# Gated delta-net: q and k normalised while v is projected, first decays early, TensorE past a barrier

## The reference

```
proj = h @ w_in                                  # h is rms-normed, 1024 wide
qkv = silu(causal_conv(proj[:, :4096], 4 taps))  # q 8 heads, k 8 heads, v 16 heads of 128
q = l2_norm(q) * 128 ** -0.5; k = l2_norm(k)     # x * rsqrt(sum(x * x) + 1e-6) over a head
beta = sigmoid(b); g = -exp(a_log) * softplus(a + dt_bias)
o = chunk_gated_delta_rule(q, k, v, g, beta)     # chunks; decay = exp(cum_i - cum_j), i >= j
out = (rms_norm(o) * silu(z)) @ w_out            # z is a further 2048 columns of proj
```

## Time and profile before

| what | value |
|---|---|
| median of three runs | 2754.71 us (2752.78 to 2757.27) |
| the profiled execution | 2757.49 us |
| its span in the profile | 2755.6 us |
| mean granted clock of TensorE | 0.931 |
| TensorE busy | 2570.0 us |
| VectorE busy | 1409.2 us |
| ScalarE busy | 849.9 us |

### The profile page before, as it was taken

How to read it: one execution, slowest core, us unless ns; L and a number is a source line. 1 busy time by engine, 2 the same in 40 slices (tenths; PEclk the granted TensorE clock), 3 DMA queues, 4 the chain that set the end, 5 groups by cost and what they waited for, 6 DMA issues and landing times.

```text
span 2755.6 us, 40042 instructions
## 1 busy us (share of the span) xinstructions
PE 2570.0 (93%) x16152; PEld 2254.5 (82%) x16152; DVE 1409.2 (51%) x1925; ACT 849.9 (31%) x1251; POOL 237.1 (9%) x186
## 2 busy tenths in 40 slices
PE   6998999888999999989997999998997788899998
PEld 6997999888999999989886888886884445688886
DVE  6676655552554443542464666766216364534433
ACT  5322443434332222322222322223223354322322
POOL 1000222220010000100100100002003100100001
PEclk9997999896999999999886999998997899899999
DMA  3222433332122222222101344543220000122221
GB/s 127 82 86 66 104 87 81 85 68 79 62 91 93 84 85 91 92 93 77 46 0 46 128 162 168 185 152 105 100 92 16 0 0 15 61 100 98 91 92 62
DMA packets 91971, 230.92 MB, mean 84 GB/s; under 512 B 59994, under 2 KB 61612, under 8 KB 67668
## 3 DMA queue, kind: packets, MB, share of 16 engines
q1 hardware_dynamic: 86320, 197.04, 22.3%
q10 hardware_dynamic: 5540, 32.30, 3.4%
HBM read 217.67 MB, written 11.64 MB: 83 GB/s over the span
## 4 chain that ended last, share of the span: by engine, by line
PE 84%; DVE 9%; ACT 3%; issue 2%; DMA 1%; DVEq 0%; ACTq 0%; POOL 0%; POOLq 0%; SPq 0%
PE ps L289 64%; PE ps L453 2%; PE ps L479 1%; PE ps L967 1%; PE ps L293 1%; PE ps L2173 1%; PE ps L950 1%; PE ps L960 1%; PE ps L2155 1%; DMA g_EC<-scr_g 1%; PE ps L1622 1%; PE ps L1623 1%; DVE a_mx L2239 1%; DVE g_tmp L1114 1%; PE ps L979 1%
## 5 line engine op out<-in xcount | busy, mean ns | idle before, releaser
L289 PE MATMUL ps<-xa_hi,whi 128*128 128x264 f32 (+1 forms) x2512 | 654.5, 320 | 44.0 <-DVE wlo L312 19.9
L289 PE MATMUL ps<-xa_lo,whi 128*128 128x264 f32 (+1 forms) x2512 | 650.3, 318 | 0.0
L289 PE MATMUL ps<-xa_hi,wlo 128*128 128x264 f32 (+1 forms) x2512 | 648.9, 318 | 0.0
L312 DVE TENSOR_TENSOR wlo<-raw,whi 128x2048 fp32r<-128x2048 f32 x161 | 370.6, 2302 | 257.7 <-ACT whi L305 257.7
L289 PEld LDWEIGHTS ps<-xa_hi,whi 128*128 128x128 f32 x2512 | 418.6, 191 | 86.1 <-issue 32.5
L305 ACT ACTIVATE whi<-raw 128x2048 fp32r<-128x2048 f32 x161 | 307.5, 1910 | 581.4 <-PE ps L289 577.0
L289 PEld LDWEIGHTS ps<-xa_hi,wlo 128*128 128x128 f32 x2512 | 417.7, 191 | 29.8
L289 PEld LDWEIGHTS ps<-xa_lo,whi 128*128 128x128 f32 x2512 | 417.7, 191 | 29.3
L289 PE MATMUL ps<-xb_hi,whi 128*128 128x264 f32 (+1 forms) x1280 | 385.3, 342 | 7.4 <-DVE xb_lo L1739 5.6
L289 PE MATMUL ps<-xb_lo,whi 128*128 128x264 f32 (+1 forms) x1280 | 386.1, 342 | 0.0
L289 PE MATMUL ps<-xb_hi,wlo 128*128 128x264 f32 (+1 forms) x1280 | 384.3, 341 | 0.0
(11 more groups left out here) (387 smaller groups left out, 2954.1 us busy)
## 6 DMA issues: line engine op xcount, KB each, us to landing
raw<-weights SPq DMA_DIRECT2D x161, 1024.0 KB, 4.9
mod_w<-weights_mod ACTq DMA_DIRECT2D x24, 1024.0 KB, 4.9
g_EC<-scr_g SPq DMA_DIRECT2D x10, 424.0 KB, 5.1
scr_z<-z_st SPq DMA_DIRECT2D x16, 264.0 KB, 4.6
g_D<-scr_g SPq DMA_DIRECT2D x10, 371.0 KB, 5.1
scr_a<-g_AT SPq DMA_DIRECT2D x10, 318.0 KB
h<-x_in ACTq DMA_DIRECT2D x4, 528.0 KB, 8.1
z_a<-scr_z SPq DMA_DIRECT2D x4, 528.0 KB, 4.9
```

The source lines that it names most:

```text
L289: mm = pe.matmul(ps[:, at_ + step * c + bank, 0:tn], w[:, hb.slot, k, c * P:(c + 1) * P], x[:, k, t0:t0 + tn], start=(k == 0 and n == 0), ...
L312: dve.tensor_tensor(wlo[:, hb.slot], raw[:, hb.raw_slot], whi[:, hb.slot].bitcast(F32), ALU.subtract).then_inc(S("w_lo"), 1)
```

## The change

The l2 norm is no step of its own any more. Its statistics (`dve_l2_stats`) stand behind the first half block of v, (4,0); its transposes (`pe_l2_rows`) in the middle of the second tile of (4,1); its roots (`act_l2_roots`) behind (4,1), and the low part (`dve_l2_low`) ahead of (5,0). The 16 columns of the identity are copied at once into `head_one`. From the tile (5,0,1) to (7,0,0) each projection tile has a slot of two heads behind it on TensorE (`pe_l2_tiles`); VectorE multiplies the two heads (`dve_l2_tiles`) right behind the evacuation of the next projection tile. The loops over v's half blocks are written out. ScalarE issues the masks' DMAs behind the roots, and ends the first step with the decays of half 0 and the split of half block 18, whose VectorE part moves behind `matrices(0)`. GpSimd clears its tiles early and ends the first step with the differences of half 0. TensorE doesn't wait at the first barrier (`join=st.n > 0`): it goes on with kk(0) and two z half blocks and waits behind them. SyncE's first transfers for the delta rule stand ahead of the load of half block 18, and the load of 19 behind `blocks_in(0)`.

Left out below are the removal of the turn-0 cases in `pe_headnorm` and `dve_headnorm` (`head_all` and `head_out` raised by two), a wait for the norm ahead of the masks' DMAs, and `decays` and `differences` under their new names `act_row_decays` and `pool_differences`, otherwise the same.

```diff
--- before.py
+++ after.py
@@ -152,7 +152,8 @@
         misc = con.take("misc", [P, 8])
         stat = con.take("stat", [P, 8])
         head_stat = con.take("head_stat", [P, 96])
-        head_st = [con.take(f"head_st{c}", [P, 8], F32R) for c in range(2)]
+        head_one = con.take("head_one", [P, 16], F32R)
+        head_st = [head_one[:, 8 * c:8 * c + 8] for c in range(2)]
         xa_hi = at("xa_hi", [P, KT, T], SB_XA, F32R)
         xa_lo = at("xa_lo", [P, KT, T], SB_XA + X_BYTES, F32R)
         xb_hi = at("xb_hi", [P, KT, T], SB_XB, F32R)
@@ -234,10 +235,15 @@
...
-            def end(self):
+            def end(self, join=True):
 
                 self.eng.drain().then_inc(S("stage_" + self.name), 1)
                 self.n += 1
+                if join:
+                    self.join()
+
+            def join(self):
+
                 for other in ENGINES:
                     if other != self.name:
                         self.eng.wait_ge(S("stage_" + other), self.n)
@@ -666,8 +668,10 @@
             return HalfBlock(HB_GDN_IN, i, 2).after(s) if not isinstance(i, int) else HalfBlock(HB_GDN_IN + 2 * i + s)
 
         def pe_gdn_in(pe):
-            def project(i, s):
-                pe_hb(pe, gdn_hb(i, s), xa_hi, xa_lo, FULL, "conv_x", i * 4 + 2 * s)
+            pe.sem_inc(S("head_all"), 2)
+
+            def project(i, s, during=None, between=None):
+                pe_hb(pe, gdn_hb(i, s), xa_hi, xa_lo, FULL, "conv_x", i * 4 + 2 * s, during=during, between=between)
 
             def sums(i, s, ahead=0):
 
@@ -689,10 +693,63 @@
             pe_gdn_gates(pe)
             project(HALF_IN, 0)
             sums(HALF_IN, 1, ahead=4)
-            project(HALF_IN, 1)
-            with pe.Fori(HALF_IN + 1, 2 * HALF_IN) as i:
-                project(i, 0)
-                project(i, 1)
+            project(HALF_IN, 1, during=((1, KT // 2), lambda: pe_l2_rows(pe)))
+            for i in range(HALF_IN + 1, 2 * HALF_IN):
+                for s in range(2):
+                    project(i, s, between=lambda: pe_l2_tiles(pe, i, s, 0))
+                    pe_l2_tiles(pe, i, s, 1)
+
+        L2_FIRST = 4 * HALF_IN + 5
+
+        def l2_tiles(i, s, c):
+
+            slot = 4 * i + 2 * s + c - L2_FIRST
+            return range(2 * slot, 2 * slot + 2) if 0 <= slot < 8 else ()
+
+        def pe_l2_rows(pe):
+            chunks, size = token_chunks(FULL)
+            pe.wait_ge(S("head_inv"), 2)
+            for j, (bank, a, _) in enumerate(chunks):
+                mm = pe.transpose(ps[0:16, 6 + bank, a:a + size], head_stat[0:size, 16 * j:16 * j + 16], ident[0:size, 0:size])
+            mm.then_inc(S("head_rows"), 1)
+
+        def pe_l2_tiles(pe, i, s, c):
+            pe.wait_ge(S("head_lo"), 1)
+            pe.wait_ge(S("head_st"), 16)
+            for n in l2_tiles(i, s, c):
+                pe.wait_ge(S("head_out"), n + 1)
+                for bank, t0, tn in FULL:
+                    for part in l2_roots[1:]:
+                        mm = pe.matmul(ps[:, 4 + 2 * (n % 2) + bank, 0:tn], head_one[0:16, n:n + 1].to_broadcast([16, P]), part[0:16, t0:t0 + tn],
+                                       start=part is l2_roots[1], stop=part is l2_roots[2])
+                mm.then_inc(S("head_all"), 1)
+
+        def act_l2_roots(act):
+            act.activation(head_one[0:16, :], ident[0:16, 0:16], ACT.Copy).then_inc(S("head_st"), 16)
+            act.wait_ge(S("head_rows"), 1)
+            for to in l2_roots[:2]:
+                act.activation(cols(to[0:16], FULL), ps[0:16, 6:8, 0:T // 2], ACT.Sqrt).then_inc(S("head_rstd"), 1)
+
+        def dve_l2_stats(dve):
+            chunks, size = token_chunks(FULL)
+            x = head_stat[0:size, 0:16 * len(chunks)]
+            dve.sem_inc(S("head_out"), 2)
+            dve.wait_ge(S("head_sums"), 16)
+            dve.tensor_scalar(x, ps[0:size, 4, 0:16 * len(chunks)], 1.0, EPS, ALU.mult, ALU.add).then_inc(S("head_inv"), 1)
+            dve.wait_ge(S("head_inv"), 1)
+            dve.reciprocal(x, x).then_inc(S("head_inv"), 1)
+
+        def dve_l2_low(dve):
+            root_, hi, lo = (x[0:16] for x in l2_roots)
+            dve.wait_ge(S("head_rstd"), 2)
+            dve.tensor_tensor(lo, root_, hi.bitcast(F32), ALU.subtract).then_inc(S("head_lo"), 1)
+
+        def dve_l2_tiles(dve, i, s, c):
+            for n in l2_tiles(i, s, c):
+                x = cols(qkv[:, n], FULL)
+                dve.wait_ge(S("head_all"), n + 3)
+                dve.scalar_tensor_tensor(x, x, prm("l2_gain", n), ps[:, 4 + 2 * (n % 2):6 + 2 * (n % 2), 0:T // 2], ALU.mult, ALU.mult)\
+                    .then_inc(S("head_out"), 1)
 
         def act_gdn_in(act):
             act.sem_inc(S("conv_silu"), 2)
@@ -724,11 +781,14 @@
...
-            with act.Fori(HALF_IN, 2 * HALF_IN - 1) as i:
+            for i in range(HALF_IN, 2 * HALF_IN):
                 for s in range(2):
-                    convolved(i, s, False)
-            for s in range(2):
-                convolved(2 * HALF_IN - 1, s, False, split=s == 0)
+                    convolved(i, s, False, split=(i, s) != (2 * HALF_IN - 1, 1))
+                    if (i, s) == (HALF_IN, 1):
+                        act_l2_roots(act)
+                        act_gdn_masks(act)
+            act_row_decays(act, 0)
+            act_split(act, HalfBlock(HB_GDN_OUT + 1))
 
         def dve_gdn_in(dve):
             dve.sem_inc(S("conv_out"), 2)
@@ -740,12 +800,14 @@
...
-            def convolved(i, s, split=True):
+            def convolved(i, s, split=True, also=None):
                 hb = gdn_hb(i, s)
                 for c in range(2):
                     dve.wait_ge(S("tiles_done"), hb.index * 2 + (c + 1))
                     dve.wait_ge(S("conv_out"), i * 4 + (2 * s + c + 1))
                     dve.tensor_tensor(cols(conv_in[:, c, 3:], FULL), pair(c, FULL), cols(rstd, FULL), ALU.mult).then_inc(S("conv_x"), 1)
+                    if also:
+                        also(c)
                     dve.wait_ge(S("conv_x"), i * 4 + (2 * s + c + 3))
                     dve.wait_ge(S("conv_silu"), i * 4 + (2 * s + c + 1))
                     for j in range(4):
@@ -768,11 +830,13 @@
...
-            with dve.Fori(HALF_IN, 2 * HALF_IN - 1) as i:
+            for i in range(HALF_IN, 2 * HALF_IN):
                 for s in range(2):
-                    convolved(i, s)
-            for s in range(2):
-                convolved(2 * HALF_IN - 1, s, split=s == 0)
+                    if (i, s) == (HALF_IN + 1, 0):
+                        dve_l2_low(dve)
+                    convolved(i, s, split=(i, s) != (2 * HALF_IN - 1, 1), also=(lambda c: dve_l2_tiles(dve, i, s - 1 + c, 1 - c)) if i > HALF_IN else None)
+                    if (i, s) == (HALF_IN, 0):
+                        dve_l2_stats(dve)
 
 
         def by_chunk(x):
@@ -984,27 +1049,30 @@
...
+            pe.wait_ge(S("head_out"), 16 + 2)
+            pe.wait_ge(S("conv_x"), 32 + 2)
             kk(0)
             for n in range(Z_EARLY):
                 z_block(n)
+            join()
...
@@ -1045,10 +1113,9 @@
...
-            decays(0)
             scaled(0)
             act_split(act, HalfBlock(HB_GDN_OUT + 2))
-            decays(1)
+            act_row_decays(act, 1)
             scaled(1)
@@ -1184,6 +1251,7 @@
             dve.sem_inc(S("z_ev"), 2)
             dve.wait_ge(S("in"), IN_FIRST + 32)
             matrices(0)
+            dve_split(dve, HalfBlock(HB_GDN_OUT + 1))
             z_out(0, 0)
@@ -1197,6 +1265,14 @@
...
+        def pool_differences(pool, t):
+            if t == 0:
+                pool.wait_ge(S("in"), IN_FIRST + 32)
+            pool.wait_ge(S("g_cum"), 16 * (t + 1))
+            for x in range(2):
+                d = heads4(g_D[t % 2], x)
+                pool.tensor_tensor(d, d, g_neg[0:CH, None, :].to_broadcast([CH, 4, CH]), ALU.add).then_inc(S("g_dif"), 1)
+
@@ -1278,7 +1346,6 @@
...
-            next_load(HB_GDN_OUT + 1)
             sp.wait_ge(S("gates_a"), 8)
@@ -1288,13 +1355,15 @@
...
             sp.wait_ge(S("g_set"), 16 * (N_BLK + 3))
+            sp.wait_ge(S("w_lo"), HB_GDN_OUT)
             cum_rows(0)
-            next_load(HB_GDN_OUT + 2)
+            next_load(HB_GDN_OUT + 1)
             for name in ENGINES:
-                sp.wait_ge(S("stage_" + name), 2)
+                sp.wait_ge(S("stage_" + name), 1)
             decay_rows(0)
             blocks_out(0)
             blocks_in(0)
+            next_load(HB_GDN_OUT + 2)
@@ -2318,9 +2387,9 @@
...
-                lambda: (pool_gdn_gates(pool), pool_norm(pool, 0, FULL)),
-                lambda: (pool.memset(g_diag[:, :, :], 0.0).then_inc(S("set"), 1), pool.memset(qkv[:, :, T:TP], 0.0).then_inc(S("set"), 1),
-                         pool.memset(g_S[:, :, :], 0.0).then_inc(S("set"), 1)),
+                lambda: (pool_gdn_gates(pool), pool_norm(pool, 0, FULL), pool.wait_ge(S("gates_z"), 2),
```

(14 more changed lines are left out.)

35 lines of the change are left out of this document (13 added, 22 removed).

## The result

| | before | after |
|---|---|---|
| median of the comparison (7 runs each), us | 2757.55 (2752.78 to 2763.97) | 2771.91 (2770.26 to 2779.36) |
| ratio | | 1.0055 (1.0041 to 1.0070) |
| profiled execution, us | 2757.49 | 2770.26 |
| its span, us | 2755.6 | 2768.5 |
| last projection tile of v ends, us | 241.09 | 279.07 |

The forecast was 2766.6 with a range of 2756 to 2774. The times shown ahead of it had a median of 2754.71; times the ratio that is 2769.9. The sign, the range and the place were right; the size was too small. The medians of the table differ by 14.4 us; the ratio makes it 15.2. At the place itself the change costs 318.38 - 301.46 = 16.9 us, where the forecast had 11.9.

The account below looks back on a forecast made before the run. TensorE, busy for 93% of the span, was taken as the bound. Slots and smaller terms less the hole gave +4.4 us, z's clock +1.1, slot clock drops +6.4: +11.9 on 2754.71, so 2766.6, range 2756 to 2774.

Parts of the forecast that it names:

- The hole: Between v's last projection tile and z: 32.54 us without projection, 10.2 left because z waits for z_ev, 22.3 saved.
- its rival: At the barrier before z: TensorE really passes with two z blocks, z starts 8.4 us earlier, 2759; chance 0.04.
- Transposes, head_lo, first slot: Added inside the projection: six transposes about 0.6 us, idle wait for head_lo 2.3 with restart, first slot's matmuls 1.0.
- The slots' mechanism: Seven later slots in v's projection: VectorE evacuates before multiplying, so TensorE stalls; 3.26 us each, 22.8 in all.
- 14 with 14 us: Sign in TensorE's waits: the multiplication in dve_l2_tiles as releaser about 14 times, some 14 us in all, longest near 1.7.
- The clock in the slots: Seven slots of v's projection: four clock drops of 1.6 us taken, +6.4 us, between bounds of 0 and 12.
- v half longer by 26 to 34 us: Sign in the changed profile: the projection's v half grows by that much.
- The two rows of 1.8 us: Earlier trace: idle times of 1.80 and 1.86 us in a dense stream left the clock at 1.00, the cost 0 bound.
- The upper end: Upper bound of the slots' clock cost: each of seven slots loses 1.7 us to a drop, 12 us.
- the second rival: Slots in v's projection stall and each drops the clock: +17.5 us, 2772; chance 0.17.
- The clock at z's start: Restart of the clock at z behind 8 us of idle time: +1.1 us.
- Everything moves rigidly after z: Behind z's two blocks the rest, such as the delta rule's first half, shifts unchanged, with no gain or loss.

Follow-up runs that it names:

- z_ev early: Changed kernel with VectorE giving z_ev's first two counts where it enters v's half, not behind its barrier: 2765.65 us, ratio 1.0045 to the kernel before.
- filled gaps: Changed kernel with twelve dense matmuls that nobody reads on TensorE ahead of each of the seven slot waits: 2760.06 us, ratio 1.0018 to the kernel before.
- every engine joins: Changed kernel with TensorE waiting at the first barrier like the other engines: 2774.68 us, ratio 1.0060 to the kernel before.
- head_lo where it is used: Changed kernel with TensorE's waits for head_lo and head_st only where a slot has heads: 2767.19 us, ratio 1.0039 to the kernel before.
- pure gaps: Changed kernel without the 56 spreading matmuls of slots 1 to 7, the waits kept: 2769.01 us, ratio 1.0063 to the kernel before.

## Where the prediction was right, and where not

- **The hole** (right). Forecast: 10.2 left of 32.54, z behind z_ev. Measured: 10.05, released by L1251. The timeline of ScalarE, beside the earlier trace rows, has the steps of that sum:
```profile
282.84 0.64 ACT L765 ACTIVATE qkv<-conv_acc 128x528 f32<-128x528 f32 x1 [4.12 <-DVE conv_acc L820]
283.50 1.28 ACT L1072 ACT_TABLE_LOAD   x1
284.80 2.30 ACT L1072 ACTIVATE g_D<-g_D,g_tok 106x106 f32<-106x106 f32 x8
287.00 1.89 ACT L311 ACTIVATE whi<-raw 128x2048 fp32r<-128x2048 f32 x1
```
  Silu done 4.4 after the tile, table load 1.28, Exps 2.3, split 1.89, as taken from before. By the Trainium skill, "ScalarE: Activation LUTs", section "What ACT_TABLE_LOAD costs", a switch of tables takes about 2.66 us, of which 1.28 are the load and 1.38 a drain. The rows of after agree on the load, 1.28, and show no drain: the silu ends 0.02 ahead of it and the Exps start 0.02 behind it. The experiment with z_ev early bears out where the release sits and also the price of its rival (forecast 1.7 us of waiting behind block 18's split; it is 2.5 with the decay matrices).
- **Transposes, head_lo, first slot** (right in kind). Measured 0.46 for 0.6, 1.90 for 2.3, 1.15 for 1.0.
- **The slots' mechanism** (right). VectorE evacuates first; undone by one moved call, it gives 24.4 us back at the opening. The size: 3.26 was forecast for each, 2.9 to 3.2 and the lost overlap of 0.2 were measured, 22 us for the seven where the sum had 22.8. TensorE resumes 1.56 after the tile, not 1.70: the step read as evacuation, 0.75 from the earlier trace rows, was the distance to an instruction that reads what was just written; the multiplication, which doesn't read it, starts 0.62 after the evacuation does. That this is the reason isn't shown. And TensorE's waits show 7 with 10.9 us in all where 14 with 14 us were named: the second multiplication ends 2.1 after the tile, and by then the first four matmuls are just through.
- **The clock in the slots** (wrong in size). The step that failed is "I take four drops of 1.6: +6.4". All seven slots dropped it, six at 1.3 to 1.5 and one at 2.6: 11.4 us; the run with filled gaps measures it alone as 11.6. With that the sign "v half longer by 26 to 34 us" was missed too: it is 37.5. The two rows of 1.8 us that I weighed against it were no bound at all: in the profile of after the gap at the same place in the code, just as long, did drop the clock (below). The upper end was the right one to take, and the second rival (each slot drops the clock, 2772) names what happened, its 12 us being nearly the 11.4. The rule of the Trainium skill that the forecast set beside this ("TensorE: Matmul & The Clock Gate", section "A second HAM failure mode: psum-queue depth-cycling": a clock that swings between its levels when matmul groups have small idle times between them) agrees with the trace of after, whose granted clock goes 0.57, 1.00, 0.50 over the first two stalled slots.
- **The clock at z's start** (right). +1.4 for +1.1.
- **Everything moves rigidly after z** (right, with noise). The opening is 16.9 later, the span 12.9, and the run of the changed kernel once more shows that such a difference comes of itself.

Sum by the steps: 11.9 forecast, 16.9 measured. The clock's term was 5.0 too small, and that is the difference. The other errors cancel: the slots, head_lo and the transposes were 1.2 too large together and the hole 0.2 too dear; z's pair was 0.3 too cheap, the start of v's half is 0.4 later, and the first slot with the overlap lost at the other boundaries is 0.6 more.

## What to carry to other kernels

When a helper's work is hooked into a loop, look at which side of the loop's own wait it stands: the release that the fast engine will ask for next must be ahead of the work that the fast engine has just released, here one moved call for some 24 us. Price a stall in a dense stream by its length plus a drop of the clock each time it comes, and take such a drop as the rule once the stalls repeat, as 34 of 35 did here (below). When an engine "passes" a barrier, search for who raises the next semaphore it needs: if that instruction stands behind the same barrier, next to nothing has passed: here 0.9 us of 8.2.

## What the runs showed of the hardware

- **A short idle time repeated in each period cost the clock nearly every time.** Five profiles have the seven gaps of 1.56 us with eight 16-row matmuls behind them (the changed kernel twice, z_ev early, every engine joins, head_lo where it is used), and 34 of the 35 gaps dropped the granted clock; pure gaps of 2.24 to 2.39 us did so in six of seven places; the same pause filled with twelve dense matmuls never. A lone gap of 1.80 us went either way. It held in the earlier trace rows; in the profile of after, at the same place in the code, it didn't (timeline of TensorE, then the window):
```profile
1225.82 0.65 PE L295 MATMUL ps<-xa_hi,whi 128*128 128x264 f32 x2 [1.80 <-DVE ml L1537]
```
```profile
1224.00:1228.00 4.00, 2.20 (x11) 2.21 (x11) 4.00 (x4) 1.91 (x1) 0.00 (x0) 0.75 0.43 127
```
- **A small store takes longer behind a large load.** z's store of 264 KB took 9.56 us behind a load of 1 MB issued 0.6 us before it on the same queue (8.07 in the same order with z_ev early), where the page of its own kernel gives 5.3 as the median and that of the changed kernel 4.1; issued ahead of the load, this store and the one behind it took 5.3 and 5.4. The store of the diagonal blocks took 6.86 instead of 3.18. Why the load holds it up (the queue's order or the shared DMA engines) no run here tells apart.
